# A macaron encoder block on one core: the state-space kernel blocks are moved behind the first injections, their direct term goes to TensorE, their store is cut in two

## The chip, the cores and the metric

One Trainium2 chip, one of its cores. The metric is device time of one execution in microseconds (us), the median of several runs. Engines: PE is TensorE, DVE is VectorE, ACT is ScalarE, POOL is GpSimd, SP is SyncE, which issues nearly all DMAs of this kernel in one written order.

## The reference, cut to what matters

```
x = x + 0.5 * swiglu(rms_norm(x))                      # 1024 x 1024, D_FF 2816
q, k, v, u = rms_norm(x) @ w_in
attn = sliding-window attention of q, k, v             # 8 heads, 64 frames a chunk, window 128
ssm:  bu = einsum(u, b_bar);  s[t] = lam_bar * s[t-1] + bu[t]     # 32 groups x 16 channels, 64 complex states
      y = Re(einsum(s, c)) + d_skip * u
      z = gelu(y);  z * sigmoid(z @ w_glu + b_glu)
x = x + concat(rms_norm(attn), rms_norm(ssm)) @ w_out
x = x + 0.5 * swiglu(rms_norm(x));  rms_norm(x)
```

All in float32. The two feed-forward halves take most of the time. The change lies in the mixer between them, in the state-space part (`ssm`).

## The kernel before, in words

The sequence of 1024 frames is cut into 128 chunks of T = 8 frames for the state-space part. With 16 channels a group, a chunk of a group is a column of 128 numbers, so `u8` holds u as 128 partitions x 32 groups x 128 chunks. Groups are worked on in four parts of 8 (b = 0 to 3). For each part:

- **I (injections)**, `inject`, line 1433: TensorE multiplies `Et` (a chunk's input to the state at its end) by `u8`: 16 products per part, 128 x 64 weights, into two banks (real, imaginary).
- **R (recurrence)**, `recurrence`, lines 2624 to 2636: DVE rotates the injections by `csn`, scans over the 128 chunks. The first add is the one that hands the banks of the injection back (`inj_taken`). R0 also waits for the last store of `u` (`u_stored` 64), since its scratch space lies in the staging tile `ust`.
- **Back-rotation**: POOL turns the scanned states of parts 0 to 2 back (lines 3164 to 3174, `state_done`), DVE those of part 3 (`b3`, `state_chain`).
- **K (kernel blocks)**, `blocks_k`, line 1407: TensorE multiplies `Bb` by `CL`: for each group the 16 x 128 block row of the response within a chunk. K0 to K3 are four pairs of blocks; each pair is 16 products with 64 x 16 weights and 128 columns, into two banks. ACT copies what lies behind the first 16 columns to `kst` (`k_out`, line 1957), DVE adds the diagonal `dgl` (the direct term `d_skip`) to the first 16 (`k_first`, line 2595). When all 8 are in `kst`, SP stores it to `k_scratch` with one DMA (line 1093), waits until that has landed, and loads the block-Toeplitz matrices `Mt` out of it, T = 8 DMAs per part, 32 in all (line 1101).
- **Y (state outputs)**, `outputs_y`, lines 1455 to 1461: for each group `Mt` times `u8`, plus `CL` times the state before the chunk (two products). Y waits for its part of `Mt` (`m_loaded`), for its states and for two banks. ACT copies the result into `u8` (`y_out`, line 1970), SP stores it to `y_scratch` (8 DMAs, line 1111), waits until they have landed, and loads it in the other order as `yT` (line 1114). ACT applies GELU (`gelu`, line 2001) and splits, DVE makes the low part (`z_low`, line 2724), and TensorE can do that part's share of the GLU products.

SP's order from the last projection on is: store of u, three `csn` loads, eight loads of u's last part, the store of `kst` and its landing, 32 loads of `Mt`, two units of `w_out` (lines 1078, 1080), then for each b the stores of y and the load of `yT`.

The order of the other engines is written out by hand as lists of letters and numbers. For TensorE, `MIXER_PE`: K, I and Y as above, T and V are the last transposes and products of attention (lines 1490, 1500), f is a fill: products of the identity with itself (line 1513) that nothing reads. For ACT, `MIXER_ACT`: k is `k_out`, C and O are read-outs of attention, W the high half of a weight unit, s the squares of the attention output, y and g are `y_out` and `gelu`. For DVE, `MIXER_DVE`: d is `k_first`, R, b, a (adds of squares), z, and W (the low half of a weight unit, which waits for ACT's). Bank numbers come from `LATE_BANKS`, in the order of the K, I and Y entries of TensorE's list; a bank is waited for until its previous user was read out (`round_free`).

Of the kernel before, what the change touches and what calls it, by code (L numbers as in the profile page):

```python
# [23 lines left out]
ALU = mybir.AluOpType  # L24
ACT = mybir.ActivationFunctionType
AX = mybir.AxisListType

P = 128
# [13 lines left out]
GH = 16  # L42
NS = 64
NJ = NG // 2
T = P // GH
# [86 lines left out]
def steps(text):  # L132
    return [(s[0], int(s[1])) for s in text.split()]
# [13 lines left out]

WITH_DVE = steps("A0 w8 A1 B0 B1 A2 w9 A3 B2 A4 B3 A5 B4 W0 A6 B5 A7 B6 B7")

MIXER_PE = steps("K0 K1 V6 K2 K3 I0 T7 I1 V7 I2 f0 I3 f1 Y0 f2 Y1 Y2 Y3")  # L150
MIXER_ACT = steps("k0 k1 k2 k3 O6 k4 k5 k6 k7 C7 O7 W1 s0 s1 s2 s3 s4 s5 s6 s7 y0 y1 g0 W2 y2 g1 y3 g2 g3")
MIXER_DVE = steps("d0 d1 d2 d3 d4 d5 d6 d7 R0 W1 R1 R2 R3 b3 a0 a1 z0 z1 W2 z2 z3")

ROUND = [((kind, 2 * b + i) if kind == "K" else (kind, b), 0 if kind == "K" else i)
         for kind, b in sum((WITH_PE[o] for o in sorted(WITH_PE)), []) + MIXER_PE if kind in "KEIY"
         for i in range(1 if kind == "E" else 2)]
# [1 line left out]

STATE_STEPS = 4 * 5 + 8

EARLY_BANKS, LATE_BANKS = [5, 6, 7], [6, 7, 5, 0, 1, 6, 7, 5, 0, 1, 6, 7, 5, 0, 1, 6, 7, 4, 5, 0, 1, 6, 7, 4]

# [3 lines left out]
def in_bank(o):  # L168
    return o % 4 if o < LATE_IN else (7, 5, 6)[(o - LATE_IN) % 3]


def round_number(kind, b, i=0):
    return ROUND.index(((kind, b), i))


def bank_of(n):
    return EARLY_BANKS[n % 3] if n < N_EARLY else LATE_BANKS[n - N_EARLY]


def round_bank(kind, b, i=0):  # L180
    return bank_of(round_number(kind, b, i))
# [229 lines left out]
def by_chunk(tile):  # L411
    return tile.rearrange("p (n q) -> p n q", q=CHUNK)


def att_tile(q, g, h):

    return q[:, h * 8:(h + 1) * 8, g, :]
# [9 lines left out]
def block_kernel(nc, x, ff1_norm, ff1_w_gate, ff1_w_up, ff1_w_down, mix_norm, w_in, sink, a_re, a_im,  # L427
# [11 lines left out]
    def at(name, off, shape, dt=F32):  # L439
        return nc.alloc_sbuf_tensor_at(name, shape, dt, offset=base + off)  # L440
# [78 lines left out]
    kst = at("kst", 16 * KB, [GH, NG, P])  # L519
# [3 lines left out]
    dgl = at("dgl", 178 * KB, [GH, NG, GH])  # L523
# [4 lines left out]
    def small(name, shape, dt=F32):  # L528
        t = at(name, off[0], shape, dt)
        n = 4  # L530
        for s in shape[1:]:
            n *= s
        off[0] += (n + 31) // 32 * 32
        return t

    ident = small("ident", [P, P])
# [119 lines left out]
    bank = [ctx.enter_context(nc.psum_tensor(f"bank{i}", [P, HALF], F32)) for i in range(8)]  # L656
# [10 lines left out]
    def sem(name):  # L667
        return ctx.enter_context(nc.semaphore(name))
# [86 lines left out]
    e_taken = sem("e_taken")  # L755
    k_ready = sem("k_ready")
    k_taken = sem("k_taken")
    k_act = sem("k_act")
    diag_chain = sem("diag_chain")
    k_stored = sem("k_stored")  # L760
    m_loaded = [sem(f"m_loaded{i}") for i in range(2)]
# [84 lines left out]
    def _(sp):  # L846
# [224 lines left out]
        def load_out_unit(n):  # L1071

            u = U_OUT + n
            n = OUT_COLS[n]
            sp.wait_ge(w_lo_done, u - RS + 1)
            for kv in range(NKV):
                src = w_out[0][kv * GQ * HD:(kv + 1) * GQ * HD, n * P:(n + 1) * P]
                sp.dma_start(as3(u)[kv * HD:(kv + 1) * HD, 0:4, :],
                             src.rearrange("(g d) m -> d g m", d=HD)).then_inc(raw_loaded[u % RS], 16)
            sp.dma_start(as3(u)[:, 4:8, :],  # L1080
                         w_out[0][DA:, n * P:(n + 1) * P].rearrange("(k p) m -> p k m", p=P)
                         ).then_inc(raw_loaded[u % RS], 16)
# [5 lines left out]
            load_csn(b)  # L1088
        load_u8(3)
        k_v = k_d.rearrange("g h c -> h g c")  # L1090
        sp.wait_ge(k_taken, 8)
        sp.wait_ge(zero_stored, 48)
        sp.dma_start(k_v[:, :, (T - 1) * GH:], kst[:, :, :]).then_inc(k_stored, 16)
        sp.wait_ge(k_stored, 16)

        for b in range(4):
            if b >= 2:
                sp.wait_ge(m_loaded[b % 2], 16 * T)
            for t in range(T):
                c0 = (T - 1 - t) * GH  # L1100
                sp.dma_start(Mt[t * GH:(t + 1) * GH, 8 * b:8 * b + 8, :],
                             k_v[:, 8 * b:8 * b + 8, c0:c0 + P]).then_inc(m_loaded[b % 2], 16)

        load_out_unit(0)
        load_out_unit(1)
        y_v = y_d.rearrange("(g h) t c -> t h g c", h=GH)
        for b in range(4):
            gs = slice(8 * b, 8 * b + 8)
# [34 lines left out]
    def _(pe):  # L1143
# [216 lines left out]
        def round_free(kind, b, i=0):  # L1360

            n = round_number(kind, b, i)
            before = [m for m in range(n) if bank_of(m) == bank_of(n)]
            if not before:
                if bank_of(n) < 2:
                    pe.wait_ge(s_biased, 16)
                elif bank_of(n) == 4:
                    pe.wait_ge(o_taken, 8)
                else:
                    pe.wait_ge(v_taken, 4)  # L1370
                return
            if before[-1] < N_EARLY <= n:

                pe.wait_ge(proj_taken, max(o for o in range(2 * N_IN) if in_bank(o) == bank_of(n)) + 1)
                return
            (kind, b), i = ROUND[before[-1]]
            if kind == "K":
                pe.wait_ge(k_taken, b + 1)
            elif kind == "E":
                pe.wait_ge(e_taken, b + 1)  # L1380
            elif kind == "I":
                pe.wait_ge(inj_taken, b + 1)
            else:
                pe.wait_ge(y_taken, 2 * b + i + 1)
# [12 lines left out]
        def blocks_k(p):  # L1397

            if p == 0:
                pe.wait_ge(cl_loaded, 16)  # L1400
            for g2 in range(2):
                round_free("K", 2 * p + g2)
            for jj in range(4):
                for ri in range(2):
                    for g2 in range(2):
                        r = slice(g2 * NS, (g2 + 1) * NS)
                        last = nc.tensor.matmul(bank[round_bank("K", 2 * p + g2)][0:GH, jj * P:(jj + 1) * P],
                                                Bb[r, ri, 4 * p + jj, :], CL[r, ri, 4 * p + jj, 0:P],
                                                start=ri == 0, stop=ri == 1)
                        if jj == 3 and ri:  # L1410
                            last.then_inc(k_ready, 1)

        def transposes_e(b):

# [90 lines left out]

        def fill(i):

            if i < 2:
                pe.wait_ge(o_taken, 8)
            else:  # L1510
                pe.wait_ge(y_taken, 2)
            for n in range((20, 24, 8)[i]):
                nc.tensor.matmul(bank[4][:, 0:P], ident[:, :], ident[:, :], start=True, stop=True)  # L1513

        step = {"K": blocks_k, "E": transposes_e, "I": inject, "Y": outputs_y,
# [21 lines left out]

        for kind, b in MIXER_PE:
            step[kind](b)
# [103 lines left out]
    def _(act):  # L1643
# [307 lines left out]
        def k_out(b):  # L1951

            act.wait_ge(k_ready, b + 1)
            j0, g2 = 4 * (b // 2), b % 2
            dst = kst[:, :, :].rearrange("p (j g) m -> p g j m", g=2)[:, g2, j0:j0 + 4, GH:]
            src = bank[round_bank("K", b)][0:GH, :].rearrange("p (j m) -> p j m", j=4)[:, :, GH:]
            act.activation(dst, src, ACT.Copy).then_inc(k_act, 1)

        def e_out(b):
            act.wait_ge(e_ready, b + 1)  # L1960
# [56 lines left out]
        for o, (n, h) in enumerate(IN_ORDER):  # L2017
            act.wait_ge(proj_out, o + 1)
            src = bank[in_bank(o)][:, :]
            what, i = IN_WHAT[n]  # L2020
            if what == "u":
                if i and h == 0:
                    act.wait_ge(u_stored, 16 * i)
                dst = ust[:, :, h * 64:(h + 1) * 64]
                src = src.rearrange("p (c t) -> p t c", t=T)
            elif what != "q":
                dst = {"k": kTp, "v": vTp}[what][:, CHUNK + h * HALF:CHUNK + (h + 1) * HALF]
            else:
                dst = att_tile(qT, i, h)
                src = by_chunk(src)  # L2030
# [7 lines left out]

        for kind, b in MIXER_ACT:
            step[kind](b)  # L2040
# [10 lines left out]
        for kind, *at_ in GATED:  # L2051
# [10 lines left out]
            else:  # L2062
                i = at_[1]
# [64 lines left out]
    def _(dve):  # L2128
# [455 lines left out]
                          dsk[:, :].unsqueeze(2).to_broadcast([GH, NG, GH]), ALU.mult).then_inc(diag_chain, 1)  # L2584
        dve.wait_ge(diag_chain, 1)

        def k_first(b):

            dve.wait_ge(k_ready, b + 1)
            dve.wait_ge(k_act, b + 1)  # L2590
            j0, g2 = 4 * (b // 2), b % 2
            dst = kst[:, :, :].rearrange("p (j g) m -> p g j m", g=2)[:, g2, j0:j0 + 4, 0:GH]
            dg = dgl[:, :, :].rearrange("p (j g) m -> p g j m", g=2)[:, g2, j0:j0 + 4, :]
            src = bank[round_bank("K", b)][0:GH, :].rearrange("p (j m) -> p j m", j=4)[:, :, 0:GH]
            dve.tensor_tensor(dst, src, dg, ALU.add).then_inc(k_taken, 1)

        sc = [0]

        def step(ins):
# [119 lines left out]
        def z_low(k):  # L2719
            if k == 0:  # L2720
                dve.wait_ge(ssq_done, adds_before(N_SSM))
            for h in range(2):
                dve.wait_ge(z_hi, 2 * k + h + 1)
                dve.tensor_tensor(hT_lo[:, 4 + k, hs(h)], yT[:, k, hs(h)], hT_hi[:, 4 + k, hs(h)].bitcast(F32),  # L2724
                                  ALU.subtract).then_inc(z_lo, 1)

        mixer_step = {"d": k_first, "R": recurrence, "A": maxima, "B": normalise, "z": z_low, "b": back_rotation,
                      "a": add_squares, "w": split_in, "W": split_later}
        for kind, b in WITH_DVE + MIXER_DVE:
            mixer_step[kind](b)  # L2730

        for kind, *at_ in GATED:
# [9 lines left out]
            elif kind == "A":  # L2742
                i = at_[1]
# [498 lines left out]
```

## Time and profile before

| | us |
|---|---|
| median of 3 runs | 1668.55 (1663.08 to 1670.61) |
| profiled execution | 1671.44 |
| its span | 1669.8 |
| PE busy | 1629.0 (98%) |
| DVE busy | 1096.2 (66%) |
| ACT busy | 719.7 (43%) |
| POOL busy | 529.9 (32%) |

The span is the stretch between the first and the last recorded instruction; the profiled execution is 1.6 us longer than it. The rows of the next but one section give a start and a length in us, counted from the span's start. TensorE runs at one of two clocks; PEclk is the granted one, 1.00 being 2.4 GHz and 0.50 being 1.2 GHz. A float32 product is recorded as two matmuls, so "x32" at line 1433 is 16 products.

### The profile page before, as it was taken

The page shows a single profiled execution, that of the slowest core. Times are in us where ns is not written, and L with a number is a line of the kernel's source. Part 1 is how long each engine was busy: PE and PEld are TensorE (multiplying, and loading weights), DVE is VectorE, ACT ScalarE, POOL GpSimd, SP SyncE. Part 2 cuts the span into 40 slices and gives each one's busy share as a digit, 9 for nine tenths or more (in the row PEclk, how much of TensorE's full clock was granted, in tenths as well). Part 3 has the DMA queues.
Part 4 walks back from the last instruction along what each step waited for, and adds up shares of the span by engine and source line. Part 5 has one row for each costly group of instructions (what it writes and reads, how often), then busy time and mean ns, then how long its engine had stood idle before and what let it go on. Part 6 is the DMA issues. An engine that isn't in the chain of part 4 may idle for free.

```text
span 1669.8 us, 22192 instructions
## 1 busy us (share of the span) xinstructions
PE 1629.0 (98%) x7644; PEld 1339.9 (80%) x7644; DVE 1096.2 (66%) x1711; ACT 719.7 (43%) x1317; POOL 529.9 (32%) x953
## 2 busy tenths in 40 slices
PE   7999999999999999999998999999999999999998
PEld 5778888888888888787876788788888888888886
DVE  5866667667678878425675557756666565678765
ACT  6444344333434445336535334543333444344442
POOL 4004788877766875200143232000000000000011
PEclk8999999999999999999978999999999999999999
DMA  6345334433596544712454134233233332885443
GB/s 210 125 101 105 114 115 154 145 114 114 196 349 201 162 108 114 245 61 86 124 129 146 29 106 168 84 106 102 101 101 118 133 103 95 274 303 154 120 111 123
DMA packets 158536, 231.65 MB, mean 139 GB/s; under 512 B 18784, under 2 KB 97248, under 8 KB 154848
## 3 DMA queue, kind: packets, MB, share of 16 engines
q1 hardware_dynamic: 155360, 222.66, 41.5%
q0 software_dynamic: 3072, 7.62, 2.4%
q8 instruction: 62, 1.02, 0.3%
q14 instruction: 42, 0.34, 0.1%
HBM read 156.09 MB, written 74.15 MB: 138 GB/s over the span
## 4 chain that ended last, share of the span: by engine, by line
PE 88%; DVE 6%; ACT 2%; issue 2%; DMA 1%; POOL 1%; SPq 0%; POOLq 0%; DVEq 0%; ACTq 0%
PE bank L1146 27%; PE bank L1147 27%; PE bank L1148 27%; DVE hblo L2255 1%; PE bank L1455 1%; DVE ws_lo L2219 1%; PE bank L1513 1%; DVE htmp L2166 1%; PE bank L1310 1%; PE bank L1458 1%; PE bank L1477 1%; PE bank L1500 0%; ACT hT_hi L1679 0%; PE bank L1490 0%; PE bank L1433 0%
## 5 line engine op out<-in xcount | busy, mean ns | idle before, releaser
L1146 PE MATMUL bank<-hbhi,ws_lo 128*128 128x512 f32 x1056 | 414.0, 392 | 8.9 <-DVE ws_lo L2219 4.9
L1148 PE MATMUL bank<-hbhi,ws_hi 128*128 128x512 f32 x1056 | 411.9, 390 | 0.0
L1147 PE MATMUL bank<-hblo,ws_hi 128*128 128x512 f32 x1056 | 411.9, 390 | 0.0
L2819 POOL TENSOR_TENSOR ssq<-ssq,sqt 128x512 f32<-128x512 f32 x25 | 37.9, 1515 | 670.0 <-ACT sqt L1663 668.7
L1146 PEld LDWEIGHTS bank<-hbhi,ws_lo 128*128 128x128 f32 x1056 | 198.8, 188 | 56.1 <-issue 6.7
L1146 PE MATMUL bank<-d_hi,ws_lo 128*128 128x512 f32 x616 | 240.7, 391 | 0.0
L1148 PE MATMUL bank<-d_hi,ws_hi 128*128 128x512 f32 x616 | 239.8, 389 | 0.0
L1147 PE MATMUL bank<-d_lo,ws_hi 128*128 128x512 f32 x616 | 239.6, 389 | 0.0
L1148 PEld LDWEIGHTS bank<-hbhi,ws_hi 128*128 128x128 f32 x1056 | 198.8, 188 | 41.3
L1147 PEld LDWEIGHTS bank<-hblo,ws_hi 128*128 128x128 f32 x1056 | 198.9, 188 | 41.2 <-issue 0.5
L1731 ACT ACTIVATE loc<-bank 128x512 f32<-128x512 f32 x160 | 95.6, 597 | 254.9 <-PE bank L1148 254.9
L1778 ACT ACTIVATE d_hi<-d_in 128x512 fp32r<-128x512 f32 x154 | 96.3, 629 | 205.5 <-DMA d_in<-b_scratch 205.4
L2219 DVE TENSOR_TENSOR ws_lo<-w_sum,ws_hi 128x512 fp32r<-128x512 f32 x160 | 114.6, 716 | 97.9 <-ACT ws_hi L1694 97.9
L2389 DVE TENSOR_TENSOR d_lo<-d_in,d_hi 128x512 fp32r<-128x512 f32 x154 | 112.9, 735 | 84.4 <-ACT d_hi L1778 83.9
L1146 PE MATMUL bank<-hT_hi,w_lo 128*128 128x512 f32 x320 | 131.9, 412 | 8.8 <-DVE hT_lo L2724 5.7
L1148 PEld LDWEIGHTS bank<-d_hi,ws_hi 128*128 128x128 f32 x616 | 115.6, 188 | 24.2
L1146 PEld LDWEIGHTS bank<-d_hi,ws_lo 128*128 128x128 f32 x616 | 115.7, 188 | 24.1 <-issue 0.2
L1147 PEld LDWEIGHTS bank<-d_lo,ws_hi 128*128 128x128 f32 x616 | 115.7, 188 | 23.7 <-issue 0.2
L1694 ACT ACTIVATE ws_hi<-w_sum 128x512 fp32r<-128x512 f32 x160 | 100.2, 626 | 78.8 <-PE bank L1148 59.8
L1147 PE MATMUL bank<-hT_lo,w_hi 128*128 128x512 f32 x320 | 127.4, 398 | 0.0
L1148 PE MATMUL bank<-hT_hi,w_hi 128*128 128x512 f32 x320 | 127.4, 398 | 0.0
L2219 DVE TENSOR_TENSOR ws_lo<-raw2a,ws_hi 128x512 fp32r<-128x512 f32 x82 | 56.0, 697 | 61.8 <-ACT ws_hi L1694 61.1
(304 smaller groups left out, 2633.5 us busy)
## 6 DMA issues: line engine op xcount, KB each, us to landing
b_scratch<-loc SPq DMA_DIRECT2D x42, 1024.0 KB, 7.4
d_in<-b_scratch SPq DMA_DIRECT2D x154, 256.0 KB, 3.1
raw2a<-in_ff_w_up_dram SPq DMA_DIRECT2D x44, 512.0 KB, 4.8
loc<-in_ff_w_gate_dram SPq DMA_DIRECT2D x36, 512.0 KB, 4.8
x_scratch<-xT SPq DMA_DIRECT2D x6, 2048.0 KB, 10.8
dw_lo_place<-in_ff_w_down_dram SPq DMA_DIRECT2D x8, 1024.0 KB, 7.7
xT<-x_scratch SPq DMA_DIRECT2D x8, 1024.0 KB, 6.5
x_in<-in_x_dram SPq DMA_DIRECT2D x8, 512.0 KB, 6.8
```

Of the source, the lines that this page charges most:

```text
L1146: nc.tensor.matmul(o, wl, rh, start=first, stop=False, skip_group_check=chain)
L1147: nc.tensor.matmul(o, wh, rl, start=False, stop=False, skip_group_check=chain)
L1148: return nc.tensor.matmul(o, wh, rh, start=False, stop=last, skip_group_check=chain)
L1310: last = nc.tensor.transpose(bank[X_BANK[2 * t + kh]][:, kk * P:(kk + 1) * P], x_in[t // 4][:, t % 4, k * P:(k + 1) * P], ident[:, :])
L1455: nc.tensor.matmul(o, Mt[:, 2 * j + g2, :], u8[:, 2 * j + g2, :], start=True, stop=False)
L1458: nc.tensor.matmul(o, CL[r, 0, j, GH:], tr[r, j, :], start=False, stop=False)
L1694: act.activation(as_block(ws_hi[b][:, :]), weights(n, s), ACT.Copy).then_inc(ws_hi_done, 1)
L1731: act.activation(snap[w][:, i, :], bank[inst_bank(n, role)][:, :], ACT.Copy).then_inc(snap_taken, 1)
L1778: act.activation(d_hi[q % N_SLOT][:, :], d_in[q % N_SLOT][:, :], ACT.Copy).then_inc(d_hi_done, 1)
L2219: dve.tensor_tensor(as_block(ws_lo[b][:, :]), weights(n, s), as_block(ws_hi[b][:, :].bitcast(F32)), ALU.subtract).then_inc(ws_lo_done, 1)
L2389: dve.tensor_tensor(d_lo[q % N_SLOT][:, :], d_in[q % N_SLOT][:, :], d_hi[q % N_SLOT][:, :].bitcast(F32), ALU.subtract).then_inc(d_lo_done, 1)
L2819: pool.tensor_tensor(ssq_of(norm, h), ssq_of(norm, h), sqt_of(norm, a), ALU.add).then_inc(ssq_done, 1)
```

## The change

K0 to K3 go behind I0 and I1 on TensorE (I0 is now the first thing after the projections). The diagonal `dgl` is added in PSUM by 32 products of 16 x 16 x 16 with the identity as weights, two behind each four products of K; the eight adds of DVE are gone, and ACT copies all 128 columns. `kst` is stored in two halves: the first after K1, the second after K3. SP waits for the first one's landing, then issues the second, then loads parts 0 and 1 of `Mt`, then parts 2 and 3. Fills: before, 20 products stood ahead of I3, 24 ahead of Y0 and 8 ahead of Y1; now 16, 8, 12 and 4 stand ahead of Y0, Y1, Y2 and Y3, those from Y1 on behind the read-out of Y0. Banks are given out anew.

```
-MIXER_PE = steps("K0 K1 V6 K2 K3 I0 T7 I1 V7 I2 f0 I3 f1 Y0 f2 Y1 Y2 Y3")
-MIXER_ACT = steps("k0 k1 k2 k3 O6 k4 k5 k6 k7 C7 O7 W1 s0 ... s7 y0 y1 g0 W2 y2 g1 y3 g2 g3")
-MIXER_DVE = steps("d0 d1 d2 d3 d4 d5 d6 d7 R0 W1 R1 R2 R3 b3 a0 a1 z0 z1 W2 z2 z3")
+MIXER_PE = steps("I0 T7 V6 I1 K0 V7 K1 K2 K3 I2 I3 f0 Y0 f1 Y1 f2 Y2 f3 Y3")
+MIXER_ACT = steps("C7 O6 k0 k1 O7 k2 k3 k4 k5 k6 k7 W1 s0 ... s7 y0 y1 g0 W2 y2 g1 y3 g2 g3")
+MIXER_DVE = steps("R0 R1 W1 R2 R3 b3 a0 a1 z0 z1 W2 z2 z3")
+FILL, N_FILL_ATT = (16, 8, 12, 4), 1
-EARLY_BANKS, LATE_BANKS = [5, 6, 7], [6, 7, 5, 0, 1, 6, 7, 5, 0, 1, 6, 7, 5, 0, 1, 6, 7, 4, 5, 0, 1, 6, 7, 4]
+EARLY_BANKS, LATE_BANKS = [5, 6, 7], [6, 7, 0, 1, 5, 6, 7, 5, 6, 7, 5, 6, 7, 0, 1, 5, 6, 4, 7, 0, 1, 5, 6, 4]
...
+        def store_k(i):
+            gs = slice(16 * i, 16 * i + 16)
+            sp.wait_ge(k_taken, 4 * i + 4)
+            sp.dma_start(k_v[:, gs, (T - 1) * GH:], kst[:, gs, :]).then_inc(k_stored, 16)
...
+        store_k(0)
+        sp.wait_ge(k_stored, 16)
+        store_k(1)
+        load_m(0)
+        load_m(1)
+        sp.wait_ge(k_stored, 32)
+        sp.wait_ge(m_loaded[0], 16 * T)
+        load_m(2)
+        sp.wait_ge(m_loaded[1], 16 * T)
+        load_m(3)
...
             if p == 0:
                 pe.wait_ge(cl_loaded, 16)
+                pe.wait_ge(diag_chain, 1)
...
+                for g2 in range(2):
+                    last = nc.tensor.matmul(bank[round_bank("K", 2 * p + g2)][0:GH, jj * P:jj * P + GH],
+                                            ident[0:GH, 0:GH], dgl[:, 2 * (4 * p + jj) + g2, :],
+                                            start=False, stop=True, skip_group_check=True)
+                    if jj == 3:
+                        last.then_inc(k_ready, 1)
...
-            if i < 2:
+            if i < N_FILL_ATT:
                 pe.wait_ge(o_taken, 8)
             else:
                 pe.wait_ge(y_taken, 2)
-            for n in range((20, 24, 8)[i]):
+            for n in range(FILL[i]):
...
-            dst = kst[:, :, :].rearrange("p (j g) m -> p g j m", g=2)[:, g2, j0:j0 + 4, GH:]
-            src = bank[round_bank("K", b)][0:GH, :].rearrange("p (j m) -> p j m", j=4)[:, :, GH:]
-            act.activation(dst, src, ACT.Copy).then_inc(k_act, 1)
+            dst = kst[:, :, :].rearrange("p (j g) m -> p g j m", g=2)[:, g2, j0:j0 + 4, :]
+            src = bank[round_bank("K", b)][0:GH, :].rearrange("p (j m) -> p j m", j=4)
+            act.activation(dst, src, ACT.Copy).then_inc(k_taken, 1)
```

## Rows read from the trace of the kernel before

**Rows 1.** Windows: stretch, length, busy of PE, PEld, DVE, ACT, POOL, PEclk, DMA.

```profile
811.10:838.80 27.70, 27.70 (x370) 25.09 (x370) 18.85 (x43) 11.80 (x22) 10.44 (x11) 1.00 0.71 167
...
847.00:852.10 5.10, 5.10 (x50) 4.06 (x48) 5.00 (x8) 0.00 (x0) 4.92 (x5) 1.00 0.61 139
...
854.43:863.63 9.20, 9.20 (x48) 7.41 (x48) 6.76 (x11) 3.26 (x6) 0.00 (x0) 0.50 0.49 112
...
886.17:891.90 5.73, 5.73 (x14) 4.47 (x15) 3.70 (x15) 3.45 (x6) 0.00 (x0) 0.50 0.97 413
```

**Rows 2.** Chain of waits, end of the mixer: start, length, what.

```profile
852.10 2.34 issue
...
873.00 1.09 ACT u L1970 x2
...
877.32 2.18 DMA y_scratch<-u
879.59 3.51 DMA yT<-y_scratch
883.12 1.15 ACT yT L2001 x2
...
884.82 1.30 DVE hT_lo L2724 x2
886.17 0.79 PE bank L1146
```

**Rows 3.** Timeline of POOL, back-rotation of part 2: first instruction and last.

```profile
845.01 1.27 POOL L3164 TENSOR_TENSOR btm<-csn,tr 128x512 f32<-128x512 f32 x1
...
853.85 0.48 POOL L3174 COPY mark<-unit 128x1 f32<-128x1 f32 x1
```

**Rows 4.** Timeline of SP: start of the first issue, length of all in the row.

```profile
814.84 4.26 SPq L1056 DMA_DIRECT2D u<-u_scratch  x8
820.71 0.30 SPq L1093 DMA_DIRECT2D k_scratch<-kst  x1
824.92 16.71 SPq L1101 DMA_DIRECT2D Mt<-k_scratch  x32
...
845.63 3.90 SPq L1111 DMA_DIRECT2D y_scratch<-u  x8
851.19 0.34 SPq L1114 DMA_DIRECT2D yT<-y_scratch  x1
```

**Rows 5.** Chain of waits, 811 to 832: one row for each kind of PE step.

```profile
811.17 3.60 PE bank L1407 x64
814.77 1.01 PE bank L1500 x8
...
821.28 1.03 PE bank L1490 x8
822.31 1.90 PE bank L1433 x32
...
826.82 4.66 PE bank L1513 x40
```

**Rows 6.** Timeline of DVE: last K add, R0, W1, start of R2.

```profile
820.47 0.21 DVE L2595 TENSOR_TENSOR kst<-bank,dgl 16x64 f32<-16x64 f32 x1 [0.21 <-ACT kst L1957]
821.43 0.69 DVE L2624 TENSOR_TENSOR tr<-csn,bank 128x512 f32<-128x512 f32 x1 [0.74 <-DMA csn<-cs_scratch]
...
823.95 0.69 DVE L2629 TENSOR_TENSOR tr<-tr,rtm 128x512 f32<-128x512 f32 x1
...
827.83 1.20 DVE L2132 TENSOR_TENSOR w_lo<-raw,w_hi 128x1024 fp32r<-128x1024 f32 x1
...
835.42 0.69 DVE L2624 TENSOR_TENSOR tr<-csn,bank 128x512 f32<-128x512 f32 x1
```

**Rows 7.** Timeline of ACT: two read-outs of K.

```profile
814.80 0.96 ACT L1957 ACTIVATE kst<-bank 16x448 f32<-16x448 f32 x2 [0.79 <-PE bank L1407]
```

**Rows 8.** Timeline of PE: four float32 products of one column, at full clock.

```profile
987.84 0.95 PE L1170 MATMUL bank<-ones,ssq 128*128 128x1 f32 x8
```

More of the change, by code:

```diff
@@ L148 @@
 WITH_DVE = steps("A0 w8 A1 B0 B1 A2 w9 A3 B2 A4 B3 A5 B4 W0 A6 B5 A7 B6 B7")
-MIXER_PE = steps("K0 K1 V6 K2 K3 I0 T7 I1 V7 I2 f0 I3 f1 Y0 f2 Y1 Y2 Y3")
-MIXER_ACT = steps("k0 k1 k2 k3 O6 k4 k5 k6 k7 C7 O7 W1 s0 s1 s2 s3 s4 s5 s6 s7 y0 y1 g0 W2 y2 g1 y3 g2 g3")
-MIXER_DVE = steps("d0 d1 d2 d3 d4 d5 d6 d7 R0 W1 R1 R2 R3 b3 a0 a1 z0 z1 W2 z2 z3")
+MIXER_PE = steps("I0 T7 V6 I1 K0 V7 K1 K2 K3 I2 I3 f0 Y0 f1 Y1 f2 Y2 f3 Y3")
+MIXER_ACT = steps("C7 O6 k0 k1 O7 k2 k3 k4 k5 k6 k7 W1 s0 s1 s2 s3 s4 s5 s6 s7 y0 y1 g0 W2 y2 g1 y3 g2 g3")
+MIXER_DVE = steps("R0 R1 W1 R2 R3 b3 a0 a1 z0 z1 W2 z2 z3")
+FILL, N_FILL_ATT = (16, 8, 12, 4), 1
 ROUND = [((kind, 2 * b + i) if kind == "K" else (kind, b), 0 if kind == "K" else i)
@@ L757, in block_kernel @@
     k_taken = sem("k_taken")
-    k_act = sem("k_act")
     diag_chain = sem("diag_chain")
@@ L1090, in _, with load_m @@
         k_v = k_d.rearrange("g h c -> h g c")
-        sp.wait_ge(k_taken, 8)
         sp.wait_ge(zero_stored, 48)
[L1093 to L1098, printed above, removed]
+        def store_k(i):
+            gs = slice(16 * i, 16 * i + 16)
+            sp.wait_ge(k_taken, 4 * i + 4)
+            sp.dma_start(k_v[:, gs, (T - 1) * GH:], kst[:, gs, :]).then_inc(k_stored, 16)
+        def load_m(b):
             for t in range(T):
@@ L1408, in blocks_k @@
                                                 Bb[r, ri, 4 * p + jj, :], CL[r, ri, 4 * p + jj, 0:P],
-                                                start=ri == 0, stop=ri == 1)
-                        if jj == 3 and ri:
-                            last.then_inc(k_ready, 1)
+                                                start=ri == 0, stop=False, skip_group_check=True)
+                for g2 in range(2):
[4 more added lines that the diff above has]
+                        last.then_inc(k_ready, 1)
         def transposes_e(b):
@@ L2585, in _ @@
         dve.wait_ge(diag_chain, 1)
[L2587 to L2595, printed above, removed]
         sc = [0]
@@ L2725, in z_low @@
                                   ALU.subtract).then_inc(z_lo, 1)
-        mixer_step = {"d": k_first, "R": recurrence, "A": maxima, "B": normalise, "z": z_low, "b": back_rotation,
+        mixer_step = {"R": recurrence, "A": maxima, "B": normalise, "z": z_low, "b": back_rotation,
                       "a": add_squares, "w": split_in, "W": split_later}
```

## The prediction, made before the changed kernel ran

> **What bounds the kernel now.** I read the page's busy table and clock strip first. TensorE is busy nearly throughout, but the clock strip has one dip, just past the middle, in the mixer. The windows there show it [rows 1]: the clock is full up to Y1 (5.1 us), then Y2 takes 9.2 us at half clock. It stays at half until about 891.9, where the GLU products speed up. So a dense PE is not a fast PE here.
>
> Next I read the chain of waits backwards from the GLU [rows 2]. TensorE resumes at 886.17 behind DVE's low part, behind GELU at 883.12, behind the load of `yT`(3) issued at 879.59, behind the landing of SP's eight y stores (the last takes 2.18 to land), behind ACT's read-out of Y3, which ends at 874.09. Y3 and Y2 stand before that at half clock (Y3 as long as Y2), and before Y2 a gap of 2.34 us. The POOL timeline names its cause: `state_done` 3 comes from the copy that ends at 854.33 [rows 3].
>
> Last I read SP's order [rows 4], because a store is moved in it. The `Mt` loads cost 16.71/32 = 0.52 us each to issue, 4.18 us a part. They begin when the store of `kst` has landed (824.92), end at 841.63, and with the two `w_out` units SP is free at 845.63. That was when Y0 had just been read out, so SP's own queue was close to ending last already.
>
> **The change, step by step.** Steps, at full clock [rows 5]: K 1.80 a pair, V 1.01, T 1.03, I 1.90, a fill product 4.66/20 = 0.233.
>
> *I0, T7, V6, I1 first.* Their inputs and banks are ready by 811.1 (the staging read-out for bank 7 is long done), so they run 811.1 to 816.9. K0's second bank is I0's old one, so K0 waits for R0's first add. R0 waits for the landing of the last u store, which let SP go at 814.84 [rows 4]. The add ends 823.95 + 0.69 - 821.43 = 3.21 us after R0's start [rows 6]: 818.05. So a new PE gap of 1.1 us stands in front of K0.
>
> *The added products.* 32, recorded as 64 matmuls, 16 records a K pair. The trace has none of this shape. Below: nothing, if they slip in beside the K products. Above: the one-column product with full weights, 0.95/8 = 0.119 a record, 1.9 us a pair [rows 8]. I take the rate of K's own records, 1.80/32 = 0.057, the nearest in weight width: 0.9 us, so that a K pair takes 2.7.
>
> The Trainium skill, "TensorE: Matmul & The Clock Gate", section "Back-to-back issue gap", gives a floor of about 25 ns from start to start for small products; by it, as an estimate, a pair would cost 0.4 us more, and the second K store would come 2 us earlier than in my sum. No row here shows that shape.
>
> *K against its read-outs.* K0 818.05 to 820.75, V7 to 821.8, K1 to 824.5. K2 writes the bank of K1's first block, so it waits for ACT: 0.1 us of release and half of the pair's time. Two read-outs took 0.96 for 448 columns [rows 7]; for 512 I take 1.09, as for two read-outs of Y [rows 2]. K2 825.15 to 827.85, K3 828.5 to 831.25, and `k_taken` 8 at 832.4. Before it was 820.47 + 0.21 = 820.68 [rows 6]. The second half of `kst` is thus 11.7 us later. The eight adds of DVE (0.21 each) and ACT's 0.06 a copy are no term: DVE was waiting at that place, and R0 is no longer behind them.
>
> *The store in two halves.* The first half can go at 825.6 and land by 829.8, if it takes the whole one's 4.2 us [rows 4]. But SP's next instruction is the second store, which waits for `k_taken` 8, and all `Mt` loads are queued behind it. So they start at 832.4 + 0.35 = 832.75 instead of 824.92: the split gives back only the landing of 4.2 us. Part 0 is issued by 836.9 and part 1 by 841.1; with 2.2 us to land, as for the last y store [rows 2], part 0 is there at about 839.1. The 16.7 us of issues end at 849.5, `w_out` at 853.5. The y stores of part 0 start there, 7.8 us later than before.
>
> *DVE and POOL.* R0 runs 814.85 to 821.25 (827.83 - 821.43 = 6.40) and R1 to 827.7. Then stands W1, whose high half ACT makes only behind k7, at 833.4; its low half ends at 834.5. R2 starts there, against 835.42: of the 6.6 us by which R0 is earlier, 0.9 are left. R3 ends at 847.4. POOL has parts 0 and 1 done by then and starts part 2 at about 841, not 845.01, so with its 9.3 us at most [rows 3] `state_done` 3 is at 850.3. b3 starts at 847.4 and takes the same, under 856.
>
> *Y with fills.* I2, I3 831.25 to 835.05; f0 16 x 0.233 = 3.7, to 838.8; Y0 839.1 (for `Mt`) to 844.2; read-out 1.1; f1 1.9; Y1 847.2 to 852.3; f2 2.8; Y2 855.1 to 860.2 at full clock, since the gap of 2.34 us is filled; f3 0.9; Y3 861.1 to 866.2, against 872.9. On TensorE alone the change is worth 6.7 us.
>
> *But SP ends last.* A part on SP is 851.19 - 845.63 = 5.56 to the `yT` issue, and 0.35 for it [rows 4]; a load lands 3.53 later [rows 2]. Part 0: 853.5, `yT`(0) issued 859.1, landed 862.6. ACT's list has g0 (2.1) and W2 (1.05) ahead of y2 (1.1), which so ends at 866.9. Part 1: 859.4 to 865.3. Part 2: from 866.9, when y2 is in, to 872.8. y3 stands behind g1 (`yT`(1) landed 868.6) and is in by 871.9. Part 3: 872.8, issued 878.3 (5.5), landed 881.8. Against 883.12 that is 1.3 us, and behind it everything shifts alike. GLU resumes cold as before, since TensorE still idles there (its share before the gap is done either way).
>
> Sum: 1671.4 - 1.3 = 1670.1 in terms of the profiled execution. That one lay 2.9 above the median of the runs, so the median should be 1668.55 - 1.3, about **1667**. With the ends of the added products, `k_taken` 8 moves by -3.7 or +4.0 us and SP with it: 5.0 us faster to 2.7 slower, 1664 to 1671.
>
> **The rivals.**
>
> *(a) The added products cost as much as full-width ones.* The skill's same page, section "The mechanism", says that a weight load overlaps a running product only if it targets other rows of the array. All added products use rows 0 to 15, which lie under K's first half. As a mechanism here: 1.9 us a pair, `k_taken` 8 at 836.4, SP later by 4.0, landing at 885.8, 2.7 us slower: 1671. For it: K's records come at half the spacing of a fill's (0.057 against 0.117) [rows 5], as if its two halves overlapped. Against it: only 16 columns of weights are loaded.
>
> *(b) Slower: the clock falls in the K stretch.* From 817 to 831 TensorE has only narrow products (16 of 128 columns) and three gaps (1.1, 0.65, 0.65 us). Before, it had K, V, I and T without a gap, and held the full clock [rows 1]. If the clock is at half from K2 on, K2 and K3 cost 5.4 more and I2, I3 3.8: I3 ends at 844.3. f0 takes 7.5, to 851.8. If f0 brings the clock back, the rest needs 27.1 as above (Y0 to Y3 with their fills, 839.1 to 866.2), so Y3 ends at 878.9, and read-out, stores and load (1.1 + 5.5 + 3.5) give 889.0: 5.9 slower, 1674. If it does not, the Y blocks cost 4.1 each more and the fills 5.6: about 22 on top, some 28 slower. The deciding point is a PEclk of 0.50 before f0. Against it: the largest gap is under half of the one behind which it fell.
>
> *(c) SP doesn't end last.* If the added products are free (3.7), the `Mt` issues run at the 3.90/8 = 0.49 of the y stores [rows 4] (1.0) and ACT's list holds part 2 up no more (866.9 - 865.3 = 1.6), SP is 6.3 us earlier. Then not SP but TensorE's own end as worked out above, Y3 at 866.2, is what is left: 866.2 + 1.1 + 5.5 + 3.5 = 876.3, 6.8 faster. If the GLU then also resumes at full clock, the 5.73 us at half clock [rows 1] give another 2.7: 9.5 faster, 1659.
>
> *(d) The fills don't hold the clock.* Y2 and Y3 take 9.2 each and f3 1.9: Y3 ends at 875.4, the load lands at 885.5, 2.4 slower: 1671.
>
> **How the numbers follow.** Within 0.5% is 8.3 us, about what a measurement of this kernel can tell from no change. My forecast 0.45, (a) 0.13, (b) 0.10, (c) 0.24, (d) 0.08. Faster by over 0.5%: the far end of (c) with some spread of runs, 0.16. Slower by over 0.5%: the worse form of (b) and spread, 0.08. The rest, 0.76, is the same. The range goes from the far end of (c), 1659, to the mild form of (b), 1674, with one for spread: 1659 to 1675.
>
> **What would show it.** Right: a PE gap of about 1 us before K0; SP's `Mt` issues starting over 7 us later than 824.9, straight behind `k_taken` 8; Y2 and Y3 at full clock, 5.1 us each; y stores of part 0 waiting on SP's own queue and not on ACT; DVE idle before W1; `yT`(3) landed near 882. Wrong: `k_taken` 8 before 829 or after 836 (the price of the added products), PEclk below 1.00 before 860, or the y stores following ACT's read-outs at once. An end earlier than 876 would overthrow the SP argument.

## The result, and the profile after

| | before | changed |
|---|---|---|
| median of 20 runs | 1670.01 | 1671.97 |
| lowest and highest | 1663.08, 1674.46 | 1670.02, 1673.84 |
| profiled execution | 1671.44 | 1671.92 |
| PE / DVE busy | 1629.0 / 1096.2 | 1623.5 / 1093.7 |

The ratio of changed to before is 1.0022, 95% interval 1.0012 to 1.0033: slower by about 0.2%, 2 to 5.5 us. The two profiled executions differ by 0.5 us only. The rest lies in the spread: seven of the 20 runs of before lie at 1663.1 to 1665.1 and thirteen at 1668.6 to 1674.5 (their medians 1663.5 and 1670.5); of the changed kernel all 20 lie at 1670.0 to 1673.8.

The chain of waits of the changed kernel, end of the mixer (start, length, what), answers to [rows 2]:

```profile
853.54 1.09 ACT u L1990 x2
854.63 0.14 SPq L1125
...
860.89 3.40 DMA yT<-y_scratch
864.31 1.15 ACT yT L2021 x2
...
866.50 0.95 ACT w_hi L1669
867.44 0.97 ACT u L1990 x2
868.43 0.30 SPq L1125
...
880.18 3.21 DMA yT<-y_scratch
883.41 1.15 ACT yT L2021 x2
...
885.12 1.31 DVE hT_lo L2734 x2
886.47 0.80 PE bank L1160
```

Where before PE's Y2 and Y3 stood, there are now SP's issues, their landings, and ACT's g0 and W2 ahead of y2. No state output is in it behind 853.5. GELU of the last part begins at 883.41 instead of 883.12, and the GLU resumes at 886.47 instead of 886.17.

The windows of the changed kernel (columns as in Rows 1) hold Y1, Y2, Y3, the stretch behind, and the resumed GLU:

```profile
848.35:853.40 5.05, 5.05 (x51) 4.08 (x49) 4.94 (x7) 0.00 (x0) 2.32 (x3) 1.00 0.86 132
856.18:861.22 5.04, 5.04 (x50) 4.07 (x48) 1.84 (x3) 0.00 (x0) 0.00 (x0) 1.00 0.63 133
862.22:867.26 5.04, 5.04 (x50) 4.07 (x48) 1.18 (x2) 2.95 (x5) 0.00 (x0) 1.00 0.67 186
867.26:873.40 6.14, 1.06 (x11) 1.00 (x9) 1.72 (x4) 4.30 (x9) 0.00 (x0) 0.79 0.68 171
886.47:891.50 5.03, 5.03 (x12) 4.03 (x13) 3.71 (x15) 3.03 (x6) 0.00 (x0) 0.52 1.02 436
```

The clock is held through Y3, and Y2 and Y3 take 5.04 us each, against 9.2 [rows 1]. Y3 ends at 867.3, 5.6 us earlier than before. What that bought is spent waiting: the clock falls behind it and the GLU resumes at half clock, as before.

SP's timeline of the changed kernel, against [rows 4]:

```profile
825.81 7.75 SPq L1098 DMA_DIRECT2D k_scratch<-kst  x2
833.61 16.65 SPq L1104 DMA_DIRECT2D Mt<-k_scratch  x32
...
854.26 4.92 SPq L1125 DMA_DIRECT2D y_scratch<-u  x8
860.89 0.34 SPq L1128 DMA_DIRECT2D yT<-y_scratch  x1
861.28 3.85 SPq L1125 DMA_DIRECT2D y_scratch<-u  x8
...
874.21 4.26 SPq L1125 DMA_DIRECT2D y_scratch<-u  x8
880.18 0.34 SPq L1128 DMA_DIRECT2D yT<-y_scratch  x1
```

The `Mt` issues start 8.7 us later than before and take as long. The first row spans both K stores: the second waits for the last read-out, and all of `Mt` waits behind it.

### The profile page after: what moved, and what is told of

Its sections match the earlier page's. It is cut to its first block, busy times and chain, and to the rows that moved or that the text cites. A ratio compares the mean times of both kernels' runs of the same rounds, so it can differ in the third digit from the quotient of the medians.

```text
span 1670.2 us, 22260 instructions
## 1 busy us (share of the span) xinstructions
PE 1623.5 (97%) x7684; PEld 1332.6 (80%) x7684; DVE 1093.7 (65%) x1703; ACT 719.8 (43%) x1317; POOL 530.5 (32%) x953
## 4 chain that ended last, share of the span: by engine, by line
PE 86%; DVE 7%; ACT 2%; DMA 2%; issue 2%; SPq 1%; POOL 1%; POOLq 0%; DVEq 0%; ACTq 0%
PE bank L1160 27%; PE bank L1161 27%; PE bank L1162 27%; DVE hblo L2275 1%; DVE ws_lo L2239 1%; DVE htmp L2186 1%; SPq L1125 1%; PE bank L1422 1%; PE bank L1497 1%; PE bank L1637 0%; PE bank L1184 0%; ACT hT_hi L1699 0%; DVE d_lo L2409 0%; DMA x_in<-in_x_dram 0%; PE bank L1520 0%
```

## The experiments

Medians in us. A kernel is compared with the kernel before, run beside it on the same chip; that one again showed both groups of times in each set (medians 1669.55 of 31 runs, 1669.6 of 33, 1669.4 of 17). The changed kernel was not run again in these sets; a difference to its 1671.97 crosses sets, between which the median of before moved by up to 0.6. The ratios to before make such a difference smaller in e1 (1.3 us), e4 (4.2) and e6 (2.8).

**e1: the second store between two parts of Mt.**

```
         store_k(0)
         sp.wait_ge(k_stored, 16)
-        store_k(1)
         load_m(0)
+        store_k(1)
         load_m(1)
```

> The changed kernel, with SP's second store of the kernel blocks put between the Mt loads of part 0 and part 1 instead of ahead of both. Theory Q (SP's queue ends last in the changed kernel, from the second K read-out on): the Mt loads start when the first half has landed, near 829.5 instead of 833.6, SP is free for the y stores near 850.5 instead of 854.3, and the last yT load lands 3 to 4 us earlier, near 880: 1668 to 1669 against the changed kernel's 1672. Rival P (TensorE's added products, gaps and fills are what costs): Mt isn't the limit and the time stays at 1672 within 1.

Measured: 1669.13 (12 runs, 1665.4 to 1670.9), against the changed kernel's 1671.97; the ratio to before is 1.0014 (1.0001 to 1.0027). SP's timeline of e1:

```profile
825.64 0.30 SPq L1098 DMA_DIRECT2D k_scratch<-kst  x1
828.30 4.70 SPq L1104 DMA_DIRECT2D Mt<-k_scratch  x8
833.04 0.43 SPq L1098 DMA_DIRECT2D k_scratch<-kst  x1
833.51 12.71 SPq L1104 DMA_DIRECT2D Mt<-k_scratch  x24
...
850.22 3.88 SPq L1125 DMA_DIRECT2D y_scratch<-u  x8
```

Part 0 of `Mt` fits into the wait for the last K read-out. The y stores start 4.0 us earlier, the last GELU 3.5 us earlier (879.94), and the time follows with 2.8 by the medians (1.3 by the ratios, whose intervals overlap). TensorE's order is the same to the instruction and the last load lands earlier, so SP's queue is what ended last.

**e6: one store.** The split undone in the changed kernel.

```
-        store_k(0)            # waits for 4 read-outs
-        sp.wait_ge(k_stored, 16)
-        store_k(1)            # waits for 8
+        store_k()             # all of kst, waits for 8
+        sp.wait_ge(k_stored, 16)
         load_m(0)
         load_m(1)
-        sp.wait_ge(k_stored, 32)
```

> The changed kernel with the kernel blocks stored by one DMA behind the last read-out, as before, and all Mt loads behind its landing. Theory Q: the Mt loads start some 4 us later (837.5 instead of 833.6) and everything behind them on SP with them: 1675 to 1676. Rival (Mt and SP's queue aren't the limit): 1672.

Measured: 1675.41 (8 runs), 1.0039 (1.0021 to 1.0058) of before. The store goes at 834.30 and takes 4.16 to land, the `Mt` issues start at 838.49 (4.9 later), the last GELU at 887.90 (4.5 later). The split is worth 3.4 us in the changed kernel by the medians, no more than the landing it hides. SP isn't alone on the path here: TensorE waits 4.26 us for `Mt`, its clock is at 0.53 from 845 to 850, and the stores of part 1 wait until y1 is in at 865.03, 0.8 us after SP was free.

**e4: without the 32 added products.** The products and their `stop` flags are removed; the direct term is left out of the result.

```
-                for g2 in range(2):
-                    last = nc.tensor.matmul(... ident[0:GH, 0:GH], dgl[...], start=False, stop=True, ...)
```

> The changed kernel without the 32 added products of the identity with the diagonal; the direct term d_skip is left out of the result. Theory Q: each K pair is 0.75 us shorter, the last K read-out 3.0 us earlier, and as SP's whole queue hangs on it the last yT load lands 3 us earlier: 1669. Rival (something behind Mt ends last): no change, 1672.

Measured: 1666.98 (12 runs), 5.0 below the changed kernel. PE's timeline, a pair of K without and with them, each with the step behind it; first e4:

```profile
817.69 1.92 PE L1422 MATMUL bank<-CL,Bb 64*16 64x128 f32 x32 [1.36 <-DVE tr L2635]
819.54 1.08 PE L1516 MATMUL bank<-pts,vwin 128*64 128x256 f32 x8
```

and the changed kernel:

```profile
817.74 0.61 PE L1422 MATMUL bank<-CL,Bb 64*16 64x128 f32 x8 [1.31 <-DVE tr L2639]
818.28 0.26 PE L1427 MATMUL bank<-dgl,ident 16*16 16x16 f32 x4
818.47 0.61 PE L1422 MATMUL bank<-CL,Bb 64*16 64x128 f32 x8
...
820.67 1.08 PE L1520 MATMUL bank<-pts,vwin 128*64 128x256 f32 x8
```

A pair goes from 819.54 - 817.69 = 1.85 us to 820.67 - 817.74 = 2.93: the added products cost 1.08 a pair, not 0.75 as I had read off their own rows (0.19 a step, four times). They also stretch the K products around them, 0.54 a step against 1.85/4 = 0.46. Four pairs make 4.3 us; the `Mt` issues start 4.3 us earlier (829.34), the last GELU 4.4 (878.97), the median 5.0. Again it passes through SP. With e6, the 8.7 us by which the `Mt` issues start late can be taken apart, as an estimate that adds the three up: 4.3 for the added products, 4.9 less by the split, and so 9.3 for K's later place with the gaps around it.

**e3: the changed kernel without its fills ahead of Y2 and Y3.**

```
-MIXER_PE = steps("... f0 Y0 f1 Y1 f2 Y2 f3 Y3")
+MIXER_PE = steps("... f0 Y0 f1 Y1 Y2 Y3")
```

> The changed kernel without its fills ahead of Y2 and Y3 (12 and 4 products). Theory Q: no gap stands before Y2 there (states and Mt are in by then), Y2 and Y3 come 2.8 and 3.7 us earlier at full clock, but SP's y stores don't, so the time stays at 1672 within 1. Rival P (fills on TensorE's path): 3 to 4 us faster, 1668. Rival C (the fills hold the clock): Y2 or Y3 at half clock, 1672 or more.

Measured: 1671.27 (8 runs, 1669.0 to 1674.6), no change within its spread. The clock is 1.00 up to 865 there too. In the changed kernel the last two fills neither hold the clock nor cost anything: no gap was left for them to fill.

**e2: the kernel before with fills ahead of Y2 and Y3.** K stays first, the direct term on DVE, the store whole.

```
-MIXER_PE = steps("... f1 Y0 f2 Y1 Y2 Y3")
+MIXER_PE = steps("... f1 Y0 f2 Y1 f3 Y2 f4 Y3")
-            for n in range((20, 24, 8)[i]):
+            for n in range((20, 24, 8, 10, 4)[i]):
```

> The kernel before with one edit: 10 products that nothing reads ahead of Y2 and 4 ahead of Y3; K first, direct term on DVE and the one store stay. Theory M (the kernel before has two times, near 1664 and near 1670.5, since the 2.34 us gap before Y2 takes the clock down in some executions and not in others): all executions hold PEclk 1.00 through Y3, Y2 and Y3 take 5.1 us each, the last yT load lands near 876, and all times lie near 1663 to 1664, 7 under the upper of the two. Rival (the two times come from elsewhere): a spread as before, 1664 and 1670, with or without the fills.

Measured: 1662.70 (12 runs, 1660.6 to 1665.3), a ratio of 0.998 (0.9969 to 0.9992) to before, 3.3 us; the medians differ by 6.9. The upper group is gone. The windows of e2, Y2 and Y3:

```profile
853.64:858.70 5.06, 5.06 (x49) 4.15 (x48) 4.57 (x8) 3.22 (x6) 0.00 (x0) 1.00 0.60 97
859.76:864.80 5.04, 5.04 (x50) 4.08 (x49) 1.46 (x3) 2.12 (x5) 0.00 (x0) 1.00 0.79 206
```

The last GELU starts at 875.19, 8 us before that of either kernel. This profile (1660.64) is the fastest of the 12 runs, and 2.9 us of its distance to the profile of before lie behind the last GELU (see c0 to c3). So one part of the change, done alone, is the gain, and the other parts take it away.

**c0 to c3: the kernel before, profiled four more times, and e5: a longer gap.** In e5 the fill ahead of Y1 is taken out, so that Y1 ends earlier and Y2 starts no earlier.

```
-MIXER_PE = steps("... I3 f1 Y0 f2 Y1 Y2 Y3")
+MIXER_PE = steps("... I3 f1 Y0 Y1 Y2 Y3")
```

> The kernel before, unchanged, for one more profile of it. Theory M: its times fall into two groups, near 1664 and near 1670.5, and the profile's clock belongs to its time: an execution of the lower group shows PEclk 1.00 through Y2 and Y3 and the last yT load near 876, one of the upper group 0.50 from about 854 on, as the profile shown. Rival: an execution of the lower group shows the half clock in the same place, and the 6 us come from elsewhere.

> The kernel before, unchanged, one more profile. Theory M: if its time is in the lower group (below 1667), PEclk is 1.00 through Y2 and Y3 and the last yT load lands near 875; if in the upper (1669 and more), 0.50 from Y2 on. Rival: a lower time with the half clock from Y2 on.

> The same as the run before it: one more profile of the unchanged kernel, to have one of each group.

> The same again: one more profile of the unchanged kernel, to have one of each group.

> The kernel before without its 8 fill products ahead of Y1, so that Y1 ends some 1.9 us earlier and the gap before Y2 is 4.3 us instead of 2.3. Theory M: with a longer gap the clock falls in nearly every execution, the lower group of times disappears, and the median is the upper group's, 1670 to 1671. Rival (the two groups don't hang on this gap): still two groups, 1664 and 1670.5, in like shares.

Profiled executions: c0 1669.39, c1 1664.52, c2 1667.43, c3 1670.98, e5 1670.90. The clock falls at the start of Y2 or within it in each of them, c1 too. What sets c1 apart in the mixer is that it comes back within Y3, behind its first quarter. Windows of c1: Y2 and the part of Y3 at half clock, then the rest of Y3.

```profile
853.77:864.62 10.85, 10.85 (x61) 8.71 (x61) 6.76 (x11) 5.44 (x11) 0.00 (x0) 0.54 0.43 97
864.62:868.40 3.78, 3.78 (x38) 3.18 (x36) 2.43 (x3) 0.99 (x2) 0.00 (x0) 0.97 0.81 132
```

and of c3, Y2 and Y3:

```profile
854.01:863.21 9.20, 9.20 (x48) 7.41 (x48) 6.76 (x11) 3.25 (x6) 0.00 (x0) 0.50 0.49 114
863.21:872.40 9.19, 9.19 (x50) 7.44 (x48) 2.43 (x3) 3.15 (x6) 0.00 (x0) 0.50 0.51 114
```

Theory M as I wrote it is wrong: no profile shows a lower time with the clock held through Y2. The half of it that stands is that a lower time goes with fewer us at half clock: c1's last GELU starts at 878.86, c3's at 882.63. The expectation of e5 failed as well: with a gap of 4.07 us its 12 runs still lie between 1665.0 and 1672.3 with a median of 1668.4, 5 of 12 of them below 1668, against 13 of the 33 runs of before beside them. So the longer gap didn't do away with the lower group.

From the last GELU's start to the end of the span c3 takes 786.7 us, c1 and c2 take 783.9 and 783.8, and before and the changed kernel 786.7 and 786.8. So part of the spread lies behind the place that the change touches. In all profiles here this way is either 783.8 to 783.9 (c1, c2, e2) or 786.5 to 787.0 (the others), but for e8's 784.9. Windows behind the norm sum of the state-space output, where TensorE waits 2.3 us for POOL; c3:

```profile
919.00:925.00 6.00, 6.00 (x19) 5.03 (x20) 3.51 (x15) 0.56 (x3) 0.00 (x0) 0.50 0.33 90
```

and c2:

```profile
919.00:925.00 6.00, 6.00 (x21) 4.79 (x20) 1.75 (x8) 0.00 (x0) 0.00 (x0) 0.72 0.31 90
```

There the clock falls a second time, for longer in c3: from the norm sum's first product to the next spreading products it is 13.3 us in c3 (917.88 to 931.16) and 1.6 less in c2. Another 1.2 us lie ahead of it: the clock is back 3.4 us behind the GLU's first product there in c2, and 5.9 us behind it in c3. So c1's place in the lower group has two parts, 3.8 us in the mixer and 2.8 behind it. The 12 runs of e2 lie at 1660.6 to 1662.1 and 1663.3 to 1665.3, six each, as if by this second part alone; one profile of them doesn't show it.

**e7: both bounds cut.** From the changed kernel: only I0 ahead of K0, K1 ahead of I1, e1's store order, W1 first in the lists of ACT and DVE, y2 ahead of W2, the second `w_out` unit behind part 0 of y, banks to match.

```
+MIXER_PE = steps("I0 K0 T7 K1 V6 I1 K2 V7 K3 I2 I3 f0 Y0 f1 Y1 f2 Y2 Y3")
+MIXER_ACT = steps("W1 k0 k1 k2 k3 C7 O6 k4 k5 O7 k6 k7 s0 ... s7 y0 y1 g0 y2 W2 g1 y3 g2 g3")
+MIXER_DVE = steps("W1 R0 R1 R2 R3 b3 a0 a1 z0 z1 W2 z2 z3")
+FILL, N_FILL_ATT = (12, 8, 6), 1
```

> A version meant to take both bounds away: only I0 stands ahead of K0, K1 comes before I1, the second K store goes out between the Mt loads of part 0 and part 1, W1 is first in the lists of ACT and DVE, y2 stands ahead of W2, the second w_out unit is loaded behind part 0 of y, fills of 12, 8 and 6 products ahead of Y0, Y1, Y2. Theory Q with M: SP can start the y stores near 843, the last yT load lands near 869 to 870 against 875 of e2, and Y2 and Y3 run at full clock: 1657 to 1659, all executions in one group. Rival (TensorE or the states end last once SP's queue is cut): no better than e2, 1663.

Measured: 1663.50 (11 runs, 1661.6 to 1666.3), 0.9969 (0.9956 to 0.9982) of before; one group, but no better than e2. Its last K read-out is in only at 830.0, so SP waits 1.5 us again, and the y stores start at 845.1 instead of 843. The second `w_out` unit then stands between parts 0 and 1 of y. The last GELU starts at 874.30, 0.9 us before e2's, but the way behind it is the longer one (786.7), so these two profiles can't be set against each other by their times. My sum for it was 5 us too low.

**e8: e2 with fills inside the first GLU output**, 10 and 21 products ahead of the waits for the third and fourth part of z.

```
             for k in range(4):
+                if o == 0:
+                    for _ in range((0, 0, 10, 21)[k]):
+                        nc.tensor.matmul(bank[7][:, 0:P], ident[:, :], ident[:, :], start=True, stop=True)
                 pe.wait_ge(z_lo, 2 * k + 2)
```

> e2 (the kernel before with fills ahead of Y2 and Y3) with 10 and 21 more products that nothing reads inside the first GLU output, ahead of the waits for the third and the fourth part of z. Theory M: TensorE has no idle stretch from Y1 to the GLU, the clock stays at 1.00, and the some 3 us of GLU products that e2 runs at half clock behind the last wait take half: 1.5 to 2.5 us faster than e2, 1660 to 1661. Rival (the fills end later than z, or the chain behind the GLU is ACT's and DVE's own): no change or slower, 1663 or more.

Measured: 1662.46 (12 runs, 1661.7 to 1663.8), 0.9968 (0.9955 to 0.9981) of before, and no gain over e2's 1662.70 that 12 runs can tell. PEclk is 1.00 from 875 to 890 (0.83 over 865 to 875, so the clock was not held throughout), and the way from the last GELU's start to the norm's spreading products is 6.6 us (875.69 to 882.28) instead of 8.0 (875.19 to 883.21), so 1.4 us were gained at that place; the last GELU itself starts 0.5 later. The rest is lost at the second fall of the clock. TensorE's rows there, e8:

```profile
908.58 3.20 PE L1170 MATMUL bank<-ones,ssq_y 128*128 128x1 f32 x16 [2.62 <-POOL ssq_y L3186]
921.88 1.02 PE L1178 MATMUL bank<-dgt_att,ones 128*128 128x512 f32 x2
```

and e2:

```profile
909.15 1.95 PE L1170 MATMUL bank<-ones,ssq_y 128*128 128x1 f32 x16 [2.26 <-POOL ssq_y L3183]
920.83 1.02 PE L1178 MATMUL bank<-dgt_att,ones 128*128 128x512 f32 x2
```

e8 arrives 0.6 us earlier and takes 13.3 us from the first of these rows to the second instead of 11.7: its clock is at 0.50 from 909 to 913.5, where e2's is 0.86 over 909.2 to 913.2. Both beat both kernels.

## Why the prediction was wrong

The forecast was 1.3 us faster in a range of 1659 to 1675; 1671.97 is in the range, on the other side, and the change is slower by 0.12 to 0.33%. The working against the profile after, point by point:

- **TensorE's order: right.** The gap before K0 is 1.31 (1.1 forecast), those before K2 and K3 0.72 each (0.65), and all of I3 has ended by 835.7 (835.05).
- **The added products: taken at 0.9 a pair, measured 1.08** (e4). It is inside the bounds of 0 and 1.9. Rival (a), 1.9 a pair, overstates the price, but its direction holds: the products cost more than their own rows show, since the K products beside them take 0.54 a step instead of 0.46.
- **The store in two halves: right.** The wait for the last read-out stands ahead of all `Mt` loads; they start at 833.6 (832.75). e1 and e6 show the place from both sides.
- **DVE and POOL: right.** DVE waits 6.96 us for W1, R2 starts at 835.31 (834.5), `state_done` 3 comes at 850.7 (850.3).
- **The clock through Y2 and Y3: right**, and rivals (b) and (d) didn't come: the clock is 1.00 through the K stretch and all Y. That the fills hold it there is not shown: e3 holds it without the last two.
- **SP ends last: right in kind, 1.6 us too small; this is the mis-sized term.** The y stores of part 0 start at 854.26 (853.5) and need 6.63 us to the `yT` issue where I took 5.56; the last part needs 5.97 where I took 5.5. The last load lands at 883.4, not 881.8. That makes the 1.3 us gained 0.3 us lost. Rival (c), in which SP doesn't end last, didn't come.
- **From the profiled execution to the median: this step failed.** I wrote that the profiled execution lay 2.9 above the median, so that the same 1.3 comes off the median. The changed kernel's profiled execution lies at its median (1671.92 and 1671.97). Of the 4.7 us between 1667.25, my sum, and 1671.97, this offset is 2.9, and 1.8 is the sum for the profiled execution (1.3 less forecast, 0.5 more measured). About half of the offset was three runs only: 20 runs of before have their median at 1670.01, not 1668.55. The other half is in the groups: the profile of before has Y2 and Y3 at half clock throughout, and that kernel doesn't do that each time. Where the clock comes back early (c1), its end of the mixer is 3.8 us earlier than c3's. The changed kernel has nothing of that kind left to gain in the mixer: its Y2 and Y3 run at full clock already, and Y3 ends at 867.3, 6.9 us before SP comes to part 3. So the saving that I weighed against SP's delay was there in full in the upper group only, and in c1 part of it was there before the change. Of the 3.6 us between the means of 20 runs (1668.3 and 1671.9), 1.2 is what the changed kernel lies above the upper group of before (mean 1670.7), and the other 2.4 is the lower group, which is gone. That the clock's return is what makes the lower group is shown by one profile for its part in the mixer; why the changed kernel shows no run with the shorter way behind the mixer isn't shown.

I had the spread before me: 1663.08 in three runs beside 1670.61, 7.5 us where my whole range was 16. Rivals (b), (c) and (d) ask what becomes of the time at the other clock, but all on the changed side. I also took 0.5% as about what can be told from no change; the interval of the 20 runs is 0.2% wide, and no change lies outside it.

What stays open: why the clock comes back in Y3 in some executions and not in others; whether every run of the lower group looks like c1, of which I have one profile at 1664.5 and none at 1663; and how much of the lower group is the second fall at 919, which the changed kernel has as well by place and which it may or may not pass early (none of its 20 runs lies more than 2.0 us below its median).

## What to carry to other kernels

When the runs of a kernel fall into two groups, ask first which group its profile shows, and make the sum for both: a saving that exists in one only is not the median's. Filling the gap ahead of the state outputs alone gave 3 to 7 us (e2, by ratio and by medians); moving back the work on which SP's loads wait took all of it and more, since in the 47 us from the first `Mt` issue on the queue pauses only for its own stores to land (1.7 us a part) and 1.3 us for y2: nearly every us by which its first step is late reaches the end (e1, e4, e6). If a store is cut in two, put something that only needs the first half between the two waits (e1).

## What the runs showed of the hardware that I had not expected

- In the kernel before, TensorE is busy without a gap through Y2 and Y3, 18.4 us, and the clock stays at 0.50 (c3); in c1 it comes back 10.85 us behind Y2's start, among the same products. Where the GLU resumes it comes back after 3.1 us (e2), 3.4 (c2) and 5.9 (c3). What makes the difference wasn't tried. The Trainium skill, "TensorE: Matmul & The Clock Gate", section "What's actually happening", says that activity releases the throttle; c1's trace agrees, and c3's has a dense stretch of 18.4 us in which it did not.
- In every profile here TensorE waits 2.3 us (2.6 in e8) for POOL ahead of the sums of the state-space norm, and the clock falls behind that wait; behind the 1.3 us gap ahead of K0 in the changed kernel it stays at 1.00.
- Products of 16 x 16 x 16 in float32, put between others, cost 0.27 us for every two of them (1.08/4), of which 0.08 is in the K products beside them. The Trainium skill, "TensorE: Matmul & The Clock Gate", section "Back-to-back issue gap", has a floor of about 25 ns from start to start; their own four records take 0.19 us, 0.048 each, nearly twice that.
- The eight y stores of one part took from 3.64 to 4.92 us to issue and 5.4 to 6.6 us to the next load, in one and the same kernel.
